# Low words written over the raw weights in a one-core decoder block, with one expert matrix loaded early and two gate units moved

## The reference

```python
def hybrid_mixer(x, w_in, conv_w, w_out_conv, w_out_attn, w_o, slopes):
    proj = jnp.einsum('bsd,dc->bsc', x, w_in)
    c_b, c_c, c_x, q, k, v, g_a, g_b = jnp.split(proj, SPLITS, axis=-1)
    y_conv = jnp.einsum('bsc,cd->bsd', c_b * causal_depthwise_conv(c_c * c_x, conv_w), w_out_conv)
    o = moba_attention(heads(q), heads(k), heads(v), slopes)
    y_attn = jnp.einsum('bsc,cd->bsd', o, w_out_attn)
    y = jax.nn.sigmoid(g_a) * y_conv + jax.nn.sigmoid(g_b) * y_attn
    return jnp.einsum('bsd,de->bse', y, w_o)

def reference(...):
    x = layer_norm(alpha * x + hybrid_mixer(x, ...), ln1_g, ln1_b)
    x = layer_norm(alpha * x + hierarchical_moe(x, ...), ln2_g, ln2_b)
    return x
```

## Time and profile before

| What | Value |
|---|---|
| Time, median of 3 runs | 392.43 us (391.44 to 392.86) |
| Profiled execution: time | 392.8 us |
| Profiled execution: span | 390.5 us |
| PE busy / PEld busy | 360.0 us (92%) / 284.8 us (73%) |
| DVE, ACT, POOL busy | 160.3, 137.3, 35.1 us |
| DMA | 132.81 MB, mean 340 GB/s |

### The profile page before, as it was taken

One profiled execution on the slowest core, in us unless ns is written; L12 is line 12 of the kernel. 1 busy time (PEld: TensorE's weight loads), 2 busy tenths in 40 slices (PEclk: granted clock), 3 DMA queues, 4 the chain that ended last, 5 costly groups with the idle time before them and its releaser, 6 DMA issues.

```text
span 390.5 us, 8013 instructions
## 1 busy us (share of the span) xinstructions
PE 360.0 (92%) x3331; PEld 284.8 (73%) x3331; DVE 160.3 (41%) x338; ACT 137.3 (35%) x239; POOL 35.1 (9%) x42
## 2 busy tenths in 40 slices
PE   7999999999999999999899999999499598299985
PEld 7999988999999999998757575757246356157632
DVE  3465579787465567365730303030310112011136
ACT  4563555655535444435623131313011213012012
POOL 3310000000000000001000005209520000000001
PEclk9999999999999999999999999999799899599999
DMA  8689884966758768699999999999999999999962
GB/s 288 212 271 388 310 305 161 347 215 217 271 179 303 259 190 307 203 417 414 414 376 428 426 425 424 424 424 426 429 421 406 427 427 424 426 425 426 412 244 111
DMA packets 52054, 132.81 MB, mean 340 GB/s; under 512 B 2818, under 2 KB 36626, under 8 KB 41012
## 3 DMA queue, kind: packets, MB, share of 16 engines
q1 hardware_dynamic: 51572, 131.88, 87.1%
q0 software_dynamic: 304, 0.17, 0.2%
q10 hardware_dynamic: 144, 0.26, 0.2%
HBM read 131.25 MB, written 1.05 MB: 339 GB/s over the span
## 4 chain that ended last, share of the span: by engine, by line
PE 61%; DMA 20%; SPq 8%; DVE 7%; ACT 2%; issue 1%; DVEq 0%
PE bank L1179 15%; DMA gu<-in_w_up 14%; PE bank L1473 10%; PE bank L1208 7%; PE bank L1341 6%; PE bank L1509 5%; DMA raw<-in_w_in 5%; PE bank L1424 4%; PE bank L1521 4%; SPq L448 3%; PE bank L1211 3%; SPq L417 3%; DVE wl L813 3%; PE bank L1278 1%; ACT wh L631 1%
## 5 line engine op out<-in xcount | busy, mean ns | idle before, releaser
L813 DVE TENSOR_TENSOR wl<-raw,wh 128x1024 fp32r<-128x1024 f32 x54 | 65.9, 1224 | 55.2 <-ACT wh L631 55.2
L1473 PE MATMUL bank<-gu,xg 128*32 128x256 f32 x1024 | 63.3, 408 | 18.7 <-DMA gu<-in_w_up 18.1
L631 ACT ACTIVATE wh<-raw 128x1024 fp32r<-128x1024 f32 x54 | 56.6, 1056 | 61.2 <-DMA raw<-in_w_in 24.9
L1473 PEld LDWEIGHTS bank<-gu,xg 128*32 128x32 f32 x1024 | 33.7, 117 | 45.0 <-issue 25.2
L1208 PE MATMUL bank<-xh,wh 128*128 128x256 f32 x176 | 44.2, 289 | 0.1
L1208 PE MATMUL bank<-xl,wh 128*128 128x256 f32 x176 | 43.1, 283 | 0.0
L1208 PEld LDWEIGHTS bank<-xh,wh 128*128 128x128 f32 x176 | 33.6, 191 | 2.3 <-issue 2.0
L1077 DVE TENSOR_SCALAR xg<-bank,gcol,bcol 128x128 f32<-128x128 f32 x32 | 10.9, 406 | 59.0 <-PE bank L1424 59.0
L1208 PEld LDWEIGHTS bank<-xl,wh 128*128 128x128 f32 x176 | 33.6, 191 | 0.0
L1424 PEld LDWEIGHTS bank<-pick,x1p 128*128 128x128 f32 x256 | 29.8, 192 | 1.9 <-issue 0.9
L1424 PE MATMUL bank<-pick,x1p 128*128 128x128 f32 x256 | 30.2, 276 | 0.6 <-DVE pick L1048 0.6
(11 more groups left out here) (235 smaller groups left out, 587.1 us busy)
## 6 DMA issues: line engine op xcount, KB each, us to landing
gu<-in_w_up SPq DMA_DIRECT2D x31, 1024.0 KB, 20.0
gu<-in_w_gate SPq DMA_DIRECT2D x30, 1024.0 KB, 14.9
dn<-in_w_down SPq DMA_DIRECT2D x26, 1024.0 KB, 17.8
raw<-in_w_in SPq DMA_DIRECT2D x40, 512.0 KB, 4.8
raw<-in_w_o SPq DMA_DIRECT2D x8, 512.0 KB, 4.5
raw<-in_w_out_conv SPq DMA_DIRECT2D x4, 512.0 KB, 3.9
raw<-in_w_out_attn SPq DMA_DIRECT2D x4, 512.0 KB, 4.9
gu<-in_w_gate SPq DMA_DIRECT2D x1, 2048.0 KB, 10.5
```

The costliest lines, as they stand in the source:

```text
L631: act.activation(wh[:, s, :].rearrange("p (k c) -> p k c", k=KC), raw[:, pair % NRAW, :].rearrange("p (k c) -> p k c", k=KC) [:, :, n % 2 ...
L813: dve.tensor_tensor(wl[:, s, :].rearrange("p (k c) -> p k c", k=KC), raw[:, pair % NRAW, :].rearrange("p (k c) -> p k c", k=KC) [:, :, n % ...
L1473: mm = pe.matmul(bank[6 - part][g, 0:DE], xg[:, k, g], w[:, e, part, k, :], start=(k == 0), stop=(k == KC - 1), skip_group_check=True)
```

## The change

`wl` loses its own memory and is laid over `raw`: the low words of a unit are written over its raw words, in three slots of 8 KB a partition instead of two raw slots and two slots' worth of low words. So a slot is free only when TensorE has used it (`unit_done`, not `lo_done`), and 8 KB a partition are left over, those of expert 3's up matrix in `gu1`, which is loaded early. In phase A the words are made three units ahead (`LEAD`). The gate units of chunk 3 come ahead of the second merge, so that xh and xl are free one merge earlier, and expert 0's two matrices are loaded there. The rounds are written out instead of looped on ACT.

```diff
-NRAW, NSPL = 2, 4
+NRAW, NSPL = 3, 4
...
-        raw = sb("raw", [P, NRAW, KC * GRP], where=mix_scope)
+        raw_scope = ExitStack()
+        raw = sb("raw", [P, NRAW, KC * GRP], where=raw_scope)
+        raw_scope.close()
+        wl = sb("wl", [P, NRAW, KC * GRP], F32R, mix_scope)
         wh = sb("wh", [P, NSPL, KC * P], F32R, mix_scope)
-        wl = sb("wl", [P, NSPL, KC * P], F32R, mix_scope)
...
-        sequence = (phase_a + lead
-                    + [x for j in range(JP - 1) for x in (("ga", j + 1), ("gb", j + 1), ("ca", j + 1), ("wo", j))]
-                    + [("wo", JP - 1)])
+        looped = ([x for j in range(JP - 2) for x in (("ga", j + 1), ("gb", j + 1), ("ca", j + 1), ("wo", j))][:-1]
+                  + [("ga", JP - 1), ("gb", JP - 1), ("wo", JP - 3), ("ca", JP - 1), ("wo", JP - 2)])
+        sequence = phase_a + lead + looped + [("wo", JP - 1)]
...
-        AHEAD = NSPL - 2
+        AHEAD, LEAD = NSPL - 2, NSPL - 1
...
+        def words(v, n):
+
+            return v[:, n // 2 % NRAW, :].rearrange("p (k c) -> p k c", k=KC)[:, :, n % 2 * P:(n % 2 + 1) * P]
...
                 if n >= NRAW:
-                    sp.wait_ge(lo_done, 2 * (n - NRAW + 1))
+                    sp.wait_ge(unit_done, 2 * (n - NRAW + 1))
                 load_pair(n % NRAW, *sequence[n], first=n == 0)
...
+            for i, (kind, idx) in enumerate(looped):
+                sp.wait_ge(unit_done, 2 * (PB + i - NRAW + 1))
+                load_pair((PB + i) % NRAW, kind, idx)
+                if i % 4 == 1:
+
+                    sp.wait_ge(pv_ps, CC)
+                    sp.wait_ge(zl_done, CC)
+                    load_dn_one(0, i // 4)
+                if i == 3:
+                    load_dn_one(0, QE - 1)
+                if i == 7:
+                    load_gu(1, 1, [3], parts=[1])
+            sp.wait_ge(unit_done, at("gb", JP - 1) + 2)
+            load_gu(1, 1, [0])
             n = len(sequence) - 1
-            sp.wait_ge(lo_done, 2 * (n - NRAW + 1))
+            sp.wait_ge(unit_done, 2 * (n - NRAW + 1))
             load_pair(n % NRAW, *sequence[n])
...
-            sp.wait_ge(unit_done, UNITS - 6)
-            load_gu(1, 1, [0])
-            sp.wait_ge(lo_done, UNITS - 2)
-            load_gu(1, 1, [1], parts=[0])
             sp.wait_ge(unit_done, UNITS - 4)
             load_dn_early(0)
-            sp.wait_ge(lo_done, UNITS)
             load_gu(1, 1, [1], parts=[1])
             sp.wait_ge(unit_done, UNITS - 2)
-            load_gu(1, 1, [2, 3], parts=[0])
+            load_gu(1, 1, [2])
             sp.wait_ge(acc_done, 2 * TT)
-            load_gu(1, 1, [2, 3], parts=[1])
+            load_gu(1, 1, [1, 3], parts=[0])
...
-                if 0 < n < U0 + AHEAD - NSPL:
-                    high(n + NSPL)
+                if 0 < n < U0 + AHEAD - LEAD:
+                    high(n + LEAD)
...
-                dve.tensor_tensor(wl[:, s, :].rearrange("p (k c) -> p k c", k=KC),
-                                  raw[:, pair % NRAW, :].rearrange("p (k c) -> p k c", k=KC)
-                                  [:, :, n % 2 * P:(n % 2 + 1) * P],
-                                  wh[:, s, :].bitcast(F32).rearrange("p (k c) -> p k c", k=KC),
+                dve.tensor_tensor(words(wl, n), words(raw, n),
+                                  wh[:, n % NSPL, :].bitcast(F32).rearrange("p (k c) -> p k c", k=KC),
                                   ALU.subtract).then_inc(lo_done, 1)
...
-                if n + NSPL < U0 + AHEAD:
-                    low(n + NSPL)
+                if n == 0:
+                    low(NSPL - 1)
+                elif n + LEAD < U0 + AHEAD:
+                    low(n + LEAD)
...
-            for j in range(JP - 1):
-                for i in range(UPJ):
-                    low(U0 + i + AHEAD, j)
-                    if i < 2:
-                        y_low(j, i)
-                    elif j == 1 and i < 2 + 2 * TT:
-                        add_x((i - 2) // 2, i % 2)
-                    if i >= 6:
-                        y_chunk(j + 1, i - 6, UPJ * j + U0 + 4)
+            for i in range(2 * len(looped)):
+                low(U0 + i + AHEAD)
+                for j in range(JP - 1):
+                    if i - i % 2 == (at("wo", j - 1) + 2 - U0 if j else 0):
+                        y_low(j, i % 2)
+                if i in range(UPJ + 2, UPJ + 2 + 2 * TT):
+                    add_x((i - UPJ - 2) // 2, i % 2)
+                for j in range(1, JP):
+                    if i - i % 2 == at("ca", j) + 2 - U0:
+                        y_chunk(j, i % 2, at("ca", j))
```

More of the change, by code:

```diff
@@ L620, in _, with high @@
         def _(act):
-            def high(n, j=None):
-                pair, s, more = n // 2, n % NSPL, 0 if j is None else j
+            def high(n):
+                pair, s = n // 2, n % NSPL
                 if n % 2 == 0:
-                    act.wait_ge(raw_in[pair % NRAW], more * 16 * UPJ // NRAW
-                                + 32 * (pair // NRAW + (pair % NRAW > 0)))
+                    act.wait_ge(raw_in[pair % NRAW], 32 * (pair // NRAW + (pair % NRAW > 0)))
                 if n >= NSPL:
                     by_pair = n % 2 == 0 and unit(n - NSPL)[0] == "v"
-                    act.wait_ge(unit_done, more * UPJ + n - NSPL + 1 + by_pair)
+                    act.wait_ge(unit_done, n - NSPL + 1 + by_pair)
                 act.activation(wh[:, s, :].rearrange("p (k c) -> p k c", k=KC),
-                               raw[:, pair % NRAW, :].rearrange("p (k c) -> p k c", k=KC)
-                               [:, :, n % 2 * P:(n % 2 + 1) * P], ACT.Copy).then_inc(hi_done, 1)
+                               words(raw, n), ACT.Copy).then_inc(hi_done, 1)
             def attention(i):
@@ L867, in _ @@
                     ins.then_inc(lo_done if h else first_lo, 1)
-            for n in range(2, NSPL):
-                low(n)
+            low(2)
             def scale_router():
@@ L1301, in _ @@
                 if kind == "ca":
-                    branches(n, 0, c % 2)
+                    branches(n, c % 2)
                     continue
@@ L1321, in _ @@
                         ws = slice(k * P, (k + 1) * P)
-                        for v, w in ((xh, wh), (xh, wl), (xl, wh)):
-                            mm = pe.matmul(dst, v[:, k, t * P:(t + 1) * P], w[:, s:s + 2, ws],
-                                           start=(k == 0 and v is xh and w is wh),
+                        wlow = wl[:, n // 2 % NRAW, k * GRP:(k + 1) * GRP]
+                        for v, w in ((xh, wh[:, s:s + 2, ws]), (xh, wlow), (xl, wh[:, s:s + 2, ws])):
+                            mm = pe.matmul(dst, v[:, k, t * P:(t + 1) * P], w,
+                                           start=(k == 0 and v is xh and w is not wlow),
                                            stop=(k == KC - 1 and v is xl))
@@ L1339, in merge @@
                     for h in range(2):
-                        for i, (v, w) in enumerate(((yh, wh), (yh, wl), (yl, wh))):
-                            mm = pe.matmul(bank[2 * t + h][:, :], v[:, m, t * P:(t + 1) * P],
-                                           w[:, s, h * HALF:(h + 1) * HALF],
+                        low = words(wl, n)[:, h * KHALF:(h + 1) * KHALF, :]
+                        high = wh[:, s, h * HALF:(h + 1) * HALF].rearrange("p (k c) -> p k c", k=KHALF)
+                        for i, (v, w) in enumerate(((yh, high), (yh, low), (yl, high))):
+                            mm = pe.matmul(bank[2 * t + h][:, :].rearrange("p (k c) -> p k c", k=KHALF),
+                                           v[:, m, t * P:(t + 1) * P], w,
                                            start=(j == 0 and m == 0 and i == 0), stop=True, skip_group_check=True)
@@ L1347, in merge @@
                     mm.then_inc(unit_done, 1)
[L1349 to L1359 removed]
+            for p, (kind, j) in enumerate(looped):
+                if kind == "ga":
+                    pe.wait_ge(sig_done, 2 * j)
+                if (kind, j) == ("wo", 1):
                     pe.wait_ge(seeded, 2 * TT)
                 for m in range(2):
[L1362 removed]
+                    n = U0 + 2 * p + m
+                    if kind in ("ga", "gb"):
+                        half = 0 if kind == "ga" else 1
+                        pe.wait_ge(lo_done, n + 1)
+                        product(bank[4 + m][:, half * SEQ:(half + 1) * SEQ], n, range(KC), xh, xl).then_inc(unit_done, 1)
+                    elif kind == "ca":
+                        pe.wait_ge(y_link, 2 * j + m - 1)
+                        branches(n, m)
+                    else:
+                        merge(j, n)
             pe.wait_ge(sig_done, 2 * JP)
@@ L1366, in _ @@
             for m in range(2):
-                merge(JP - 1, m, 0, m == 1)
+                merge(JP - 1, UNITS - 2 + m, m == 1)
             def transpose_tile(t):
```

72 lines of the change are left out of this document (24 added, 48 removed).

## The result

The change takes 396.29 us (median of 6 runs, 395.30 to 399.73); the kernel before, run beside it, takes 392.50 (median of 6, 391.44 to 393.00). The ratio is 1.0103, with a 95% interval of 1.0075 to 1.0131: slower by 1.0%, or 3.8 us. The forecast was 394.5, which is 2.1 us slower, with a range of 391.5 to 396.5. The time lies in the range, near its upper end; the loss is almost twice the forecast one.

What follows compares the result with a forecast made beforehand. Mixer bound by TensorE, mixture of experts by the DMA queue. -0.3 - 0.5 + 0.6 + 2.6 = +2.4 us at the mixer's end, less 0.3 old work: +2.1, so 394.5 us (range 391.5 to 396.5).

Steps and rivals of the forecast that it cites:

- same: Outcome within about 0.5%, 2.0 us, of the kernel before; chance 0.48, including half of the forecast case's 0.60.
- slower: Outcome slower than the kernel before beyond about 2.0 us; chance 0.42, including half of the forecast case's 0.60.
- late raw words: Rival, chance 0.12: pair 5's raw words land late for units 10 and 11, costing 1.3 to 3.1 us more.
- Three slots: Early mixer: earlier loads remove an ACT wait, -0.3 us, and the wait before the first head pair's probabilities, -0.5 us.
- One unit later: At unit 10, TensorE waits for low words that DVE makes behind the router's scaling: +0.6 us.
- The last merge's weights: End of mixer: weights queued behind 2 MB land at 172.9 us, so the last merge waits for y's low part, +2.6 us.
- 512 bytes for line rate: Skill's rule for the w_o transfers: two pairs at 2.4 us each, wait about 1.3 us, sum 1.3 lower; not adopted.
- Less 0.3 of old work: Behind the mixer: the DMA queue's 0.3 us of old work is gone, so +2.4 us becomes +2.1.
- The hole that I had from 183 to 186 us: Behind the mixer: sign that the forecast is right, the DMA engines pausing between 183 and 186 us.
- The early megabyte: The freed 1 MB, loaded at about 137 us where the queue is not full: free, but no help to the end.
- The weights were not in time: Denies a rival, chance 0.18: last merge's weights in time or nearly, giving 393.1 us, or 391.9 if landed by 170.3.
- bytes alone set the end: Rival, chance 0.10: the third quad's gates queue behind old bytes, the early megabyte is worth 2.5 us, giving 389.7.

Runs made afterwards that it cites:

- experiment 1: The changed kernel unaltered, run again on another chip beside the kernel before: 398.19 us, ratio 1.0135.
- experiment 4: The changed kernel with 28 unread filler matmuls on TensorE ahead of the last merge: 398.54 us, ratio 1.0138 to the kernel before.
- experiment 6: The changed kernel with only DVE's router scaling moved behind unit 11's low words: 398.41 us, ratio 1.0133 to the kernel before.
- experiment 3: The changed kernel with DVE's four last-branch sums ahead of the last merge's low words, y's low words behind each unit's: 393.23 us, ratio 1.0011.
- experiment 5: The changed kernel with 15 unread filler matmuls on TensorE ahead of the last merge: 396.06 us, ratio 1.0076 to the kernel before.
- experiment 9: The changed kernel with last merge's weights before expert 0's 2 MB, router scaling behind unit 11's low words, last-branch sums before low words: 391.84 us, ratio 0.9972.
- experiment 10: The kernel of experiment 9 without the early matrix, which goes out behind the mixer's end: 394.28 us, ratio 1.0042 to the kernel before.
- experiment 2: The changed kernel with the last merge's weights issued ahead of expert 0's two matrices: 393.64 us, ratio 1.0015 to the kernel before.
- experiment 7: The changed kernel with last merge's weights ahead of expert 0's 2 MB and router scaling behind unit 11's low words: 392.32 us, ratio 0.9992.
- experiment 11: The kernel of experiment 7 with chunk 3's gate units back behind the second merge: 393.05 us, ratio 1.0016 to the kernel before.

## Why the prediction was wrong

The chances had "same" (0.48) ahead of "slower" (0.42), because the forecast of 2.1 us lay at the edge of the 2.0 taken for noise; the interval came out at 0.3% either way, and the loss clear of it. That the time still lies in the range is luck: the upper end was put there for late raw words. At the end of the mixer the profile is 5.57 us later than before (181.79 to 187.36), where the sum had 2.4: 0.76 less from the mixer ahead of the merges, 0.97 more from the wait, and 2.96 from the merge behind it.

**Three slots (-0.3 and -0.5): right.** Neither wait is in the profile of after. With the wait of 0.3 us at unit 10 in it the mixer is 0.96 us ahead at 101.13 us, where the forecast had 0.2; 0.26 of that is an earlier first unit (8.95 against 9.21 us), on which I do not build.

**One unit later (+0.6): about right, and not constant.** It was 0.3 us in the profiled run, and 1.9 and 2.1 where the raw words of pair 5 came late (experiments 1 and 4). Moved words caused no wait after unit 12. Taking this wait away alone gave nothing measurable (experiment 6): 0.5 us at the first transposes took its place there, as the earlier trace rows have it.

**The last merge's weights (+2.6): the mechanism right, the time of day right by luck, the wait too short.** I had the weights' landing at 172.9 us, and ACT starts on them at 172.83; yl at 178.9, and the merge starts at 178.88. But TensorE was 0.96 us ahead instead of 0.2, and what releases these transfers is TensorE: the third merge's weights went out at 158.46 us, 0.94 earlier than the 159.4 of the sum. From there to ACT's start the three transfers took 14.4 us, where the sum has 13.5, so the wait was 3.6 instead of 2.6. The two errors cancelled to a tenth of a microsecond. Over the six profiles with this order the 13.5 us of the sum measured 13.4 to 15.1 (after and experiments 1, 3, 4, 5, 6); why it varies stays open. The Trainium skill (DMA: Bandwidth & Descriptors, Specifications), by whose 512 bytes for line rate the wait would have been 1.3 us shorter, is not borne out here: the transfers were slower than the sum with 340 GB/s, not faster.

**The step that failed is "a wait of 2.6 us that was not there", priced at its own length alone.** I took the merge behind it for the 5.50 us of the earlier trace rows, at the clock of every stretch of the earlier trace rows, 1.00. A waiting TensorE came out of the wait at 0.50, and the merge took 8.46 us: 2.96 us that no term of the sum holds. Experiment 5 takes away that part alone and gets 2.3 us back, with a filler that ended some 0.8 us late. The Trainium skill (TensorE: Matmul & The Clock Gate, Part 1) says that the gate falls back to half rate when TensorE idles; the rows agree here (0.50 after 3.6 us of idling), and a new wait on an engine that had none should have been read against that page. By it the forecast would have been some 3 us higher, an estimate from the measured 8.46 less 5.50.

**Less 0.3 of old work: too small to tell.** A moved by 5.57 us and Z by 5.35, but Z - A scatters by 1.0 from run to run. The hole that I had from 183 to 186 us was there, from 182 to 188, since the merge was longer. In medians the loss is 3.8 us in the result and 5.1 in experiment 1; both profiled runs are the longest of their six.

**The early megabyte: right as said, for a reason I only half had.** It did not help, because the change still leaves two matrices behind the end of the mixer, as before. A matrix more there costs 2.44 us (experiments 9 and 10), 1.05 MB at 430 GB/s. So bytes do count, but those that wait for that point.

**The rivals.** The weights were not in time. Raw words were late, but as an addition in some runs, and once with the slower clock behind the wait (experiment 4). That bytes alone set the end, the rival on the other side, is refuted by the table.

**What stays open.** Experiments 2, 7 and 11 lie within each other's intervals, so what the router's order and the order of the units are worth by themselves is not settled, nor which of the three edits brings experiment 9 below the kernel before. Why the change took 2 us more in experiment 1 than in the result, on a chip where even its lowest run was 397.94, was not tried; late raw words explain 1.6 us of one run. Nor is it shown that the clock fell in every execution of the result. Three of its six took 395.3 to 395.5 us, where the later start of the merge alone (392.5 and 2.62) would put them, and the others 397.1 to 399.7, where the slower merge (2.96 more) would; but only the longest was profiled, and the mean granted clock of a whole execution (0.964 to 0.972) does not tell the two apart.

## What to carry to other kernels

A wait put on a TensorE that had been busy without a gap can have two prices: its length, and the slower clock of what follows. In the profiled executions here waits of 2.1 and of 3.4 to 3.6 us had both, waits of 1.2, 1.5 and 1.9 us only the first. Look at the granted clock of the stretch behind it, since the busy share stays at 1. When a transfer is moved ahead, name the one that it now delays and then all the work that stands in program order behind the late one. Where the end of a phase releases transfers, count the megabytes that wait for it and the time at which it comes, and take no credit for any other byte moved early.

## What the hardware showed that I had not expected

The same 24 matmuls took 8.46, 8.40 and 8.28 us (after, experiments 1 and 6) after TensorE had waited 3.4 to 3.6 us, at a granted clock that went down to 0.50, and 5.72 us after a wait of 1.2 us (experiment 3), at 1.00 throughout:

```profile
176.10:181.90 5.80, 5.77 (x26) 4.82 (x27) 2.89 (x6) 1.81 (x4) 0.00 (x0) 1.00 0.96 383
```

The longer wait was three times as long and cost 6.6 us in all (3.6 and 2.96). The shorter cost its length alone: the merge took 5.68 us in experiment 2 too, with no wait ahead of it. (The clock also fell after the 2.14 us of experiment 4.) And matmuls that compute nothing, in a wait that cannot be shortened, kept the clock: the merge took 5.47 us behind 15 of them (experiment 5).
